# Hybrid S5 and short-convolution block: GLU sums in parts of 6 and 2, merge and output weights requested later, output projection over five token tiles

## The reference

```python
    y_s = jax.nn.gelu(y_s)
    y_s = y_s * jax.nn.sigmoid(y_s @ w_glu[l] + b_glu[l])
    y_s = y_s @ w_s_up[l]                                  # (B, L, D)
    ...
    y_c = (b_c * v) @ w_c_up[l]                            # (B, L, D)
    # gated merge + single output projection
    merged = jax.nn.sigmoid(gl_s + gb_s) * y_s + jax.nn.sigmoid(gl_c + gb_c) * y_c
    h_stream = h_stream + rms_norm(merged @ w_o[l], g_mix_post[l])
    # ---- channel-mixing sub-layer: SwiGLU (sandwich norm) ----
    h = rms_norm(h_stream, g_ffn_pre[l])
    gate, up = jnp.split(h @ w_ffn_in[l], 2, axis=-1)
    f = (jax.nn.silu(gate) * up) @ w_ffn_out[l]
    h_stream = h_stream + rms_norm(f, g_ffn_post[l])
```

## Time and profile before

| | |
|---|---|
| median of 3 runs | 1840.55 us (1840.54 to 1956.79) |
| profiled execution | 1844.34 us |
| its span, from first to last instruction, slowest core (core 1) | 1843.3 us |
| spans of the 8 cores | 1825.6 to 1843.3 us |
| instructions on core 1 | 25331 |

### The profile page before, as it was taken

The page is one execution under the profiler, slowest core; times in us unless marked ns, Lnnn a source line. Parts: engine busy times, 40 slices in busy tenths (PEclk is TensorE's granted clock), DMA queues, the critical chain, the costliest instruction groups (busy, mean ns, idle before and its releaser), DMA issues.

```text
span 1843.3 us, 25331 instructions; the slowest of 8 cores (1825.6 to 1843.3 us)
## 1 busy us (share of the span) xinstructions
PE 1766.2 (96%) x9744; PEld 848.0 (46%) x9744; DVE 701.7 (38%) x820; ACT 496.3 (27%) x948; POOL 118.0 (6%) x226
## 2 busy tenths in 40 slices
PE   3999999999999979889999999999999999999998
PEld 2664555544444434334444444444444444444443
DVE  4475999887786524425620110110110010101023
ACT  4554665545555420014420000000000000101010
POOL 0000000000001011100000000000000000000000
PEclk9999999999999989999999999999999999999999
DMA  9754444466667878974554446464555441443457
GB/s 236 192 152 103 79 82 83 78 114 133 123 118 160 182 143 190 220 167 138 182 121 80 69 80 112 69 112 80 100 98 94 69 79 33 77 81 66 91 126 243
DMA packets 87510, 219.06 MB, mean 119 GB/s; under 512 B 34080, under 2 KB 34592, under 8 KB 80832
## 3 DMA queue, kind: packets, MB, share of 16 engines
q0 software_dynamic: 31744, 121.71, 39.3%
q1 hardware_dynamic: 52480, 90.58, 16.4%
q10 hardware_dynamic: 3168, 5.15, 0.8%
HBM read 303.32 MB, written 35.72 MB: 184 GB/s over the span
## 4 chain that ended last, share of the span: by engine, by line
PE 82%; DMA 12%; DVE 2%; issue 2%; ACT 1%; SPq 1%; POOL 0%; ACTq 0%; DVEq 0%; POOLq 0%
PE ps L219 82%; DMA yr<-yc_d 5%; DMA wus<-w_in 2%; DMA wr<-w_in 2%; DMA xin<-xseq 1%; DMA gs_d<-tc 1%; DMA gT<-g_d 1%; PE ps L225 1%; SPq L213 1%; DMA gs_d<-ys 1%; DMA xr<-xseq 0%; DVE mgd L244 0%; DVE Pt L255 0%; POOL wus L213 0%; ACT Xt L235 0%
## 5 line engine op out<-in xcount | busy, mean ns | idle before, releaser
L219 PE MATMUL ps<-hN,wf 128*128 128x512 bf16 x2816 | 608.1, 379 | 0.0
L219 PEld LDWEIGHTS ps<-hN,wf 128*128 128x128 bf16 x2816 | 275.4, 98 | 331.8
L219 PE MATMUL ps<-hT,wr 128*128 128x512 bf16 (+1 forms) x1888 | 368.8, 351 | 5.3 <-DMA wr<-w_in 4.0
L219 PE MATMUL ps<-wfo,agr 128*128 128x512 bf16 x1408 | 304.1, 379 | 0.0
L241 DVE TENSOR_TENSOR agr<-ps,sgt 128x512 bf16<-128x512 f32 x88 | 60.9, 692 | 535.8 <-PE ps L219 535.8
L219 PEld LDWEIGHTS ps<-hT,wr 128*128 128x128 bf16 x1888 | 178.8, 97 | 175.9 <-issue 15.1
L219 PEld LDWEIGHTS ps<-wfo,agr 128*128 128x128 bf16 x1408 | 137.8, 98 | 166.1
L235 ACT ACTIVATE sgt<-ps 128x512 f32<-128x512 f32 x88 | 52.6, 598 | 535.0 <-PE ps L219 535.0
L219 PE MATMUL ps<-wo,mgd 128*128 128x512 bf16 x512 | 114.6, 386 | 5.6 <-DVE mgd L244 4.8
L241 DVE TENSOR_TENSOR facc<-ps,gp2a 128x512 f32<-128x512 f32 x24 | 16.6, 692 | 212.2 <-ACT sqj L235 151.4
L235 ACT ACTIVATE sqj<-ps 128x512 bf16<-128x512 f32 x32 | 19.1, 598 | 265.3 <-PE ps L219 265.3
(11 more groups left out here) (136 smaller groups left out, 1361.4 us busy)
## 6 DMA issues: line engine op xcount, KB each, us to landing
wf<-w_ffn_in POOLq DMA_DIRECT2D x88, 512.0 KB, 5.7
wr<-w_in POOLq DMA_DIRECT2D x51, 512.0 KB, 6.5
wfo<-w_ffn_out POOLq DMA_DIRECT2D x16, 1408.0 KB, 9.7
xin<-xseq SPq DMA_DIRECT2D x16, 1024.0 KB, 8.0
yc_d<-ys SPq DMA_DIRECT2D x32, 256.0 KB, 3.4
yr<-yc_d SPq DMA_DIRECT2D x32, 256.0 KB, 14.6
wo<-w_o POOLq DMA_DIRECT2D x16, 512.0 KB, 10.5
xr<-xseq SPq DMA_DIRECT2D x8, 1024.0 KB, 6.6
```

The costliest lines, as they stand in the source:

```text
L219: return lambda e: e.matmul(o, lhsT=l, rhs=r, start=st, stop=sp)
```

## The change

It has four parts.

- GLU: the first eight groups, on all eight banks, are computed for k = 0 to 5, and k = 6 and 7 are added later.
- The requests for `ws2`, `ws3`, `ws4` and for the first two `wg` wait until the last block of `gT` has landed.
- `w_o`: the third column block is requested behind `mgd` 12 to 15 (before: 8 to 11), the fourth behind the last `mgd` (before: 12 to 15); `gfpre` waits for `mgd` 15.
- Output projection: five tiles, not three, go through the column blocks together, with five `os`. From then on each finish is two tiles behind the projection. `xr` is loaded and added in two halves, each with its own request, made once the half before it has been read. There are two `xg`, and the square writes there. `os3` and `os4` lie where `ws` and `wg` were, `xg1` over the last `wg` and the first `tsm`; the feed-forward weights `wf0` to `wf4` come to lie on the same addresses.

```diff
-    for q, i in enumerate((4, 5, 6, 7, 0, 1)):
+    for q, i in enumerate((4, 5, 6, 7, 0, 1, 2, 3)):
         first[q] = (ps[i], ("ps", i))
-        glu(q // 2, q % 2, *first[q], range(7))
+        glu(q // 2, q % 2, *first[q], range(6))
...
-                glu(m, blk, pb, pk, (7,))
+                glu(m, blk, pb, pk, (6, 7))
...
-        S.dma("pool", flat(WS[wi][:]), w_s_up[m], 524288, "ws%d" % wi, writes=["ws%d" % wi])
+        late = [("gT", 7, g8) for g8 in range(8)]
+        S.dma("pool", flat(WS[wi][:]), w_s_up[m], 524288, "ws%d" % wi, reads=late if 2 <= m < 5 else [], writes=["ws%d" % wi])
...
-            S.dma("pool", flat(WG[gi][:]), w_in[32 + m], 1048576, "wg%d" % gi, writes=["wg%d" % gi])
+            S.dma("pool", flat(WG[gi][:]), w_in[32 + m], 1048576, "wg%d" % gi, reads=late if m in LATE[:2] else [], writes=["wg%d" % gi])
...
-            after = ([("gs_d", EARLY[5 + min(kq, 1)], 1)], [("g3", kq, 0)], [("mgd", 8 + kq, 0)], [("mgd", 12 + kq, 0)])[nb]
+            after = ([("gs_d", EARLY[5 + min(kq, 1)], 1)], [("g3", kq, 0)], [("mgd", 12 + kq, 0)], [("mgd", 15, 1)])[nb]
...
-    S.dma("sp", gfpre[:], gains_d[2], 1048576, "gfpre", writes=["gfpre"])
-    OS = [S.tile("os%d" % i, [128, D], F32, a) for i, a in enumerate((180416, 188608, 56384))]
+    S.dma("sp", gfpre[:], gains_d[2], 1048576, "gfpre", reads=[("mgd", 15, 0)], writes=["gfpre"])
+    OS = [S.tile("os%d" % i, [128, D], F32, a) for i, a in enumerate((180416, 188608, 56384, 35904, 44096))]
     xr = S.tile("xr", [128, D], F32, 196800)
-    xg = S.tile("xg", [128, D], BF16, 204992)
+    XG = [S.tile("xg%d" % i, [128, D], BF16, a) for i, a in enumerate((204992, 52288))]
...
-    sqo = S.tile("sqo", [128, 512], BF16, 54336)
+    sqo = S.tile("sqo", [128, 512], BF16, 209408)
...
+    def load_r(t):
+        for h in range(2):
+            hc = slice(1024 * h, 1024 * h + 1024)
+            S.dma("sp", xr[:, hc], xseq[16 + 128 * t:144 + 128 * t, hc], 524288, "xr%d" % h, writes=[("xr", h)])
+
+    load_r(0)
+
     def finish(t):
...
-        S.dma("sp", xr[:], xseq[16 + 128 * t:144 + 128 * t, :], 1048576, "xr", writes=["xr"])
...
-        S.stt(os_[:], os_[:], r1, xr[:], ALU.mult, ALU.add, D, OK + [r1k, "xr"], OK)
+        for h in range(2):
+            hc = slice(1024 * h, 1024 * h + 1024)
+            S.stt(os_[:, hc], os_[:, hc], r1, xr[:, hc], ALU.mult, ALU.add, 1024, OK[2 * h:2 * h + 2] + [r1k, ("xr", h)], OK[2 * h:2 * h + 2])
+        if t + 1 < 8:
+            load_r(t + 1)
         S.dma("sp", hs_d[128 * t:128 * t + 128, :], os_[:], 1048576, ok, reads=OK, writes=[("hs_d", t)])
-        S.act(xr[:, 0:1024].bitcast(BF16), os_[:], AF.Square, D, OK, ["xr", r2k], accum=r2)
+        S.act(xg[:], os_[:], AF.Square, D, OK, [xk, r2k], accum=r2)
...
-        for t in range(3):
+        for t in range(5):
             project(t, nb)
-    for t in range(3):
-        if t == 2:
+    for t in range(8):
+        if t >= 3 and t + 2 < 8:
             for nb in range(4):
-                project(3, nb)
-        finish(t)
-    for t in range(3, 8):
-        if t > 3:
-            for nb in range(4):
-                project(t, nb)
+                project(t + 2, nb)
         finish(t)
```

More of the change, by code:

```diff
@@ L932, in project @@
     def project(t, nb):
-        os_, ok = OS[t % 3], "os%d" % (t % 3)
+        os_, ok = OS[t % 5], "os%d" % (t % 5)
         pb, pk = bank("all")
@@ L938, in project @@
         S.tt(os_[:, 512 * nb:512 * nb + 512], pb[:], gpost[:, 512 * nb:512 * nb + 512], ALU.mult, 512, [pk, "gpost"], [(ok, nb)])
+    def load_r(t):
[3 more added lines that the diff above has]
+    load_r(0)
     def finish(t):
-        os_, ok = OS[t % 3], "os%d" % (t % 3)
-        xk = "xg"
-        S.dma("sp", xr[:], xseq[16 + 128 * t:144 + 128 * t, :], 1048576, "xr", writes=["xr"])
+        os_, ok = OS[t % 5], "os%d" % (t % 5)
+        xg, xk = XG[(t + 1) % 2], "xg%d" % ((t + 1) % 2)
         OK = [(ok, nb) for nb in range(4)]
```

## The result

| | before | after |
|---|---|---|
| median (all) | 1840.55 us | 1822.75 us |
| ratio, 95% interval | | 0.990 (0.9885 to 0.9915) |
| profiled execution | 1844.34 us | 1823.45 us |
| spans of the 8 cores | 1825.6 to 1843.3 us | 1807.9 to 1822.4 us |

The kernel is 17.8 us faster by these medians, 1.0%. The forecast was 27.5 us, and 1822.75 lies inside the range of 1807 to 1827 but outside the forecast's own 1807 to 1819.

A forecast was written before the change was run, and what follows sets the result against it. TensorE, 96% busy on core 1, was taken as the bound, so only its waits and low-clock stretches could be won: 11.8 + 11.7 + 4.8 = 28.3 us, taken as 27.5, giving 1813.0 us; own range 1807 to 1819, with two rivals 1807 to 1827.

The forecast's parts named there:

- Gain 11.8 us: GLU: parts of 6 and 2 with merge weights behind the last g win 11.8 us, bounds 14.1 and 1.2.
- second rival: GLU: the last g lands no sooner because of its own 256-byte pieces; gain 1.2 us, time 1823; chance 0.11.
- Gain 11.7 us: Merge: later w_o and gfpre requests lower the DMA share to 0.85 and win 11.7 us, between 0 and 12.4.
- first rival: Merge: stays limited by transfers, yr having only five buffers; the 11.7 us are not won, time 1824; chance 0.12.
- PE does not feel this ... Cost nothing, with 10 us of cover: Projection start: gpost landing at 14 to 18 us costs nothing, since PE returns to its first bank after 27.8 us.
- Gain 4.8 us: Output projection over five tiles: residual waits and slow matmuls, 5.7 us, go except 0.9; gain 4.8 us.
- What could be late next is VectorE: Projection finishes: VectorE is the next possible delay, with 60 us of work against PE's 76.
- third rival: Projection: finishes do not overlap, with late xr halves for most tiles; 27 us lost, time 1844; chance 0.04.
- marks for "right": Signs listed beforehand from GLU, merge and projection that would confirm the forecast, such as no second gT wait over 2 us.
- A DMA share under 0.9 in the merge: Merge: sign of a right forecast, DMA share under 0.9, with more traffic between the merge and the finishes.
- Transposes without a wait over 1 us: Projection: sign of a right forecast, no transpose waiting more than 1 us.
- PE waiting for `xg`: Projection: sign of a wrong forecast, PE waiting for wo8, gpost or xg.

The follow-up runs named there:

- e11: Kernel before with only the last eight w_o blocks and gfpre requested later in the merge; 1835.79 us.
- e4: Kernel before with GLU in parts of 6 and 2 and merge weights behind the last g; w_o, gfpre and projection as before; 1834.16 us.
- e8: Kernel before with only the merge weights ws and wg requested behind the last g, GLU still in parts of 7 and 1; 1834.68 us.
- e7: Kernel before with only the GLU split into 6 and 2 blocks, weight requests unmoved; 1840.1 us, ratio 1.0004.
- e1: Changed kernel with the output projection of before (three tiles, one xr, one xg), all other edits kept; 1823.74 us.
- e9: Changed kernel with three tiles per column block, two full residual buffers requested two tiles ahead, tile 7 using the first again; 1813.32 us, ratio 0.9855.
- e10: Changed kernel with four tiles, two full residual buffers, tile 7 reusing first residual and product buffers, later projections one tile ahead; 1815.82 us, ratio 0.9864.
- e3: Changed kernel with the residual loaded for tile 0 only and used for all eight tiles, so the output is not the layer's; 1812.83 us.
- e6: Changed kernel with three tiles per column block and a second full residual buffer, each residual requested two tiles ahead; 1821.67 us.

## Why the prediction was right and wrong

**"Gain 11.8 us", GLU: right in kind, somewhat small.** Core 1 spends 14.2 us less there (43.7 to 29.5). The steps held: block 5 was in time, the last g landed 4.2 to 4.7 us after its request (5 was taken), and no wait was left. The 0.9 us kept for a short wait, and the late start (655.0 for block 5; the first group began at 652.45), were not needed. The second rival, "the last g lands no sooner", fell: 1.2 us were named for it, 12.3 were won. Of the 12.3, the later requests alone give 9.8 and the split the rest on top of them; the prediction didn't divide it. The argument against the rival was sound, too: in the kernel before, the pieces that landed in 1.8 us were requested between 625 and 628, and POOL requested no weights from 617.6 to 631.3; those requested between 631 and 634, beside one `wo` and one `wr`, took 9.1 in the median.

The trace decides between the rule and the row at this point. Pieces on ScalarE's queue, which holds no weights, took 10.9 us with five weight blocks just requested on POOL's queue, and 4.5 with two. The Trainium skill, page "DMA: Bandwidth & Descriptors", section "Queues, rings and completion order", has the engines take turns between queues by packets; section "Issuing engines are not separate DMA queues" of the same page says that all of them share the same 16 engines and interleave. The measured 6.4 us of difference agrees with the second sentence. That a small transfer would not stand behind the weights was the prediction's own inference from the first, and it did not hold here: taking turns did not keep a 32 KB piece clear of them.

**"Gain 11.7 us", merge: right.** Core 1 spends 10.9 us less in the stage, and the first stretch of `wo` matmuls has no slow part (336 in 72.68 us, 0.216 each, where 224 took 50.08): 1.4 more, 12.3 in all. The wait for the last `mgd` is 0.50 us (1.1 was said). e11 shows that the requests named there do all of it, and e4 and e8 that without them the earlier end of the GLU brings the merge nothing: 100.3 and 100.8, against 98.1 before and 98.5 in e7. The first rival, transfers still the limit, is thereby shown for the version that lacks this edit, and excluded for the one that has it.

**"PE does not feel this ... Cost nothing, with 10 us of cover", `gpost`: right.** `gpost` landed after 13.3 us on core 1 and VectorE began on the banks at 786.72; TensorE came back to its first bank at 800.1, eight groups of 3.45 us after 772.5: 13 us of cover. In e1, with 18.2 us to land, the banks were free in time too.

**"Gain 4.8 us", projection: the step that failed.** On core 1 the time from the first `wo` matmul to the end grew by 3.6 us (1044.7 to 1048.3), on the mean of the cores by 0.3; 8 us and 5 us away from the forecast. The failing sentence is "What could be late next is VectorE". The walk through the new order priced VectorE's instructions and gave the residual halves no landing time. With a landing time such as the 6.5 us of the earlier trace rows, or the 6.6 that `xr` itself took before, it would have shown the wait: tile 2's first half is requested at 839.43, when tile 1's has been read, and is wanted 4.7 us later, at 844.15; it came at 846.65, 7.2 us after its request. The reading of the old waits was also too simple: of the 3.39 us put down to a late `xr`, the row shows 1.33 on VectorE. Before the change a finish came about every 12 us and one residual buffer was just enough (2.6 us of waits); five tiles gather the first finishes (the first three want their residual 6 us apart, at 831.7, 838.1 and 844.2), and the same single buffer becomes the bound. Adding in halves shortens what must be free, not the time that a transfer takes. The third rival had named the mechanism, "late `xr` halves for most tiles", and was given 0.04 because it was thought to come only in full: it came in part, at seven of sixteen halves and 9.0 us of TensorE's waits on core 1, 2.3 and 3.3 us on cores 0 and 4.

That five tiles bring anything by themselves is not shown: once the residual is early, three tiles and four do the same (e9 and e10, 1037.7 and 1037.3), and five do no better without the later loads (e3, 1037.1). Five with an early residual was not run.

**The sum and its basis.** That the range holds the result is luck: 1822.75 is where the first two rivals would have put it (1824 and 1823), and neither happened. The miss is 9.7 us (27.5 forecast, 17.8 measured). The slowest cores differ by 20.9, where 28.3 was summed: projection 8.0 short (-4.8 forecast, +3.2), merge 0.8 short (10.9 of 11.7), arrival 1.0 later, GLU 2.4 better; 7.4 in all. The profiled execution of before had stood 3.8 above the median and that of after 0.7 above its own, so 3.1 of the 20.9 are absent from the medians, and 0.8 had been taken off: 7.4 + 3.1 - 0.8 = 9.7. A second, smaller weakness is reading all terms on core 1. It was the slowest core because it lost most in these very stages, 43.7 and 101.3 us where the mean core spent 41.9 and 98.1; on the mean core the two gains together were 19.9 us, where 23.5 were forecast. Which core ends last is decided anew once they are gone: in the changed kernel it is one of those that reach the stage last (654.6 on core 5), and all eight then take 29.5 to 30.0 and 90.4 to 90.6 us.

**What would have shown it.** Five of the marks for "right" were seen: the first GLU group right behind `hT`, no second `gT` wait, no `wg` wait, under 2 us before the first `wo` group, more DMA between the merge and the finishes; and the last g was under 10 us. "A DMA share under 0.9 in the merge" was wrong in its first half: 1.03 in 700 to 720 and still no wait. "Transposes without a wait over 1 us" failed, and one mark for "wrong", PE waiting for `xg`, was seen; both pointed to the right stage.

## What to carry over

When work is gathered into a shorter stretch, walk each stream of transfers through it as well as each engine: the interval between two uses of a buffer must hold the request, the landing beside that stretch's other traffic, and the use. Here the residual needed a request two tiles ahead, worth 7.4 us once the end was put right (e9 against the changed kernel), and no more tiles in flight; and a second buffer is free only if nothing that follows waits for its address: on the wrong one it gave the whole gain back (e6, 1045.2). Take gains from all cores and not from the slowest, which is the slowest partly by the losses that the change takes away.

## What the runs showed of the hardware that was not expected

- A full DMA share is not by itself a wait. The merge ran at 1.03 in 700 to 720 and 1.01 in 740 to 760 without a TensorE wait; e11 shows that what had made it wait is the `w_o` and `gfpre` requests alone.
- Small transfers on a queue of their own are slowed by large ones on another: 10.9 us behind five weight blocks against 4.5 behind two, for 32 KB (e7, changed kernel).
- Cores that share no data reach the same point up to 10 us apart (644.2 to 653.6 before, 646.3 to 654.9 after), in another order in each execution. No run here tells why. So a single core of a single execution is read with some microseconds of doubt.
- Work that a fixed order puts into the same bank twice in a row costs its whole evacuation, 1.79 us, on every core and in both versions that have it (e1, e11), and on none in e9, which has three tiles too but another order.
